# Expert layers of a decoder trunk: gathered expert rows replaced by dense products over both expert tables with a sparse gate matrix

## The chip, the cores and the metric

One core of a Trainium2 chip runs the whole program in one launch. The metric is the device time of that core in microseconds (us), lower is better. All data and all products are float32.

## The reference

The input is 256 tokens of width 1024; 16 learned meta tokens go in front, so there are 272 rows, worked on as a tile of 16 and two tiles of 128. Two layers follow, each an attention and then an expert feed-forward ("PEER"). The attention parts are not what the change is about. The expert part is, cut to what matters:

```python
q = (xt @ w_q).reshape(n, 8, 2, 128)                       # 8 heads, two halves
s = jnp.einsum('nhcd,ckd->nhck', q, subkeys)               # 128 keys per half
s_top, i_top = lax.top_k(s, 16)
cand = s_top[:, :, 0, :, None] + s_top[:, :, 1, None, :]   # 16 x 16 pairs
cand_id = i_top[:, :, 0, :, None] * 128 + i_top[:, :, 1, None, :]
best, pick = lax.top_k(cand..., 16)                        # 16 experts per head
ids = ...; g = jax.nn.softmax(best, axis=-1)
act = gelu(einsum('cd,ced->ce', xc, u[ids])) * g           # u, v: (16384, 1024) per layer
out = einsum('ce,ced->cd', act, v[ids])
```

Each token picks 8 x 16 = 128 of the 16384 experts of its layer. For each pick it needs one row of `u` (a dot product with the token) and one row of `v` (added to the output with weight `act`). Each table of a layer is 64 MiB.

## The kernel before, in words

The engines run hand-written instruction streams that meet only at semaphores. Tokens of the expert part are taken in groups of 16 (`GT = 16`): 8 groups for each tile of 128 and one for the meta tokens, and since the meta tokens are not needed after layer 0, there are 17 + 16 = 33 groups. In a group, partition p stands for (head, token), 8 x 16 = 128 pairs, and the 16 picks of a pair are walked one after the other (k = 0 to 15).

For pick k of a group, GpSimd starts an indirect DMA that fetches 128 rows of `u` (one per partition, 4 KB each), and the same for `v` of the group before (`gather`, L505). The arena is a ring of 8 slots for `u` and 8 for `v`. VectorE multiplies the fetched rows with the tokens' rows and sums (`step`, L1077). ScalarE applies gelu and writes 16 diagonal-like matrices (L764), and TensorE multiplies each with the fetched rows of `v`, 2 x 512 columns per pick, into two PSUM banks (`v_sum`, L1371). In the middle of a group (k = 7, `ROUTE`) the next group is routed: TensorE makes the scores, VectorE finds the best keys and pairs (L1014 to L1064).

The other work is spread into the gaps between the picks by a table (`work`): while tile 1 of a layer is in its expert groups, tile 2's attention, output projection and query projection run, and so on across the layers. So only tile 1's attention of layer 0 stands ahead of the first group, some 140 us. The weights come in blocks of 0.5 MB through a ring of six slots on SyncE's queue.

Of the kernel before, what the change touches and what calls it, by code (L numbers as in the profile page):

```python
# [5 lines left out]
F32 = mybir.dt.float32  # L22
U32 = mybir.dt.uint32
# [8 lines left out]
TILES = 3  # L32
# [11 lines left out]
EXPERTS = 16384  # L44
NKEYS = 128
SEL = 16
GT = 16
# [8 lines left out]
WB = 6  # L56

XC = META + P

UP_STEPS = 15  # L60


class Chain:

    def __init__(self, eng, sem):
        self.eng, self.sem, self.n, self.off = eng, sem, 0, 0

    def do(self, ins):  # L70
        self.n += 1
        ins.then_inc(self.sem, 1)
        self.eng.wait_ge(self.sem, self.n + self.off)


def build(nc, x, meta, a_norm, a_w_in, a_q_norm, a_k_norm, a_w_o, kv_norm, kv_w, b_norm, b_w_q, b_w_o,
          ffn_norm, peer_w_q, peer_subkeys, peer_u, peer_v, rope, out):
    u_rows = peer_u.rearrange("l e d -> (l e) d")
    v_rows = peer_v.rearrange("l e d -> (l e) d")
    with ExitStack() as ctx:  # L80
        def sb(name, cols, dt=F32, rows=P):
            return ctx.enter_context(nc.sbuf_tensor(name, [rows, cols], dt))
# [11 lines left out]
        arena = sb("arena", 16 * D)  # L94
        ring = arena[:, :].rearrange("p (k d) -> p k d", d=D)

        w_r = arena[:, 0:KC * (A_COLS - Q_COLS)].rearrange("p (c n) -> p c n", n=A_COLS - Q_COLS)
        w_q = arena[:, 8 * D:8 * D + KC * Q_COLS].rearrange("p (c n) -> p c n", n=Q_COLS)

        wb_t = sb("weight_blocks", WB * D)  # L100
        wb = wb_t[:, :].rearrange("p (s c n) -> p s c n", s=WB, n=P)

        hx_t = sb("residual", TILES * D)
        hx = hx_t[:, :].rearrange("p (i d) -> p i d", d=D)
        x1_t = sb("x_norm_T", KC * XC)
        xT = x1_t[:, :].rearrange("p (c n) -> p c n", n=XC)
        x2_t = sb("kv_norm_T", KC * XC)
        xT2 = x2_t[:, :].rearrange("p (c n) -> p c n", n=XC)
        qt_t = sb("queries_T", 2 * 17 * P)


        QT = qt_t[:, :].rearrange("p (c g m) -> p c g m", c=2, m=P)
        QTw = qt_t[:, :].rearrange("p (c g h t) -> p c g h t", c=2, h=HEADS, t=GT)
        dg_t = sb("diagonals", 16 * P)
        DG = dg_t[:, :].rearrange("p (k m) -> p k m", m=P)
        l_t = sb("logits", GROUP * T)
        L = l_t[:, :].rearrange("p (h k) -> p h k", k=T)
        re_t = sb("index_scores_and_softplus", 2 * GROUP * T)
        r_t, e_t = re_t[:, 0:GROUP * T], re_t[:, GROUP * T:2 * GROUP * T]
        E4 = e_t.rearrange("p (h k) -> p h k", k=T)  # L120
        SC, WK = e_t[:, 0:T], e_t[:, T:2 * T]
        R4 = r_t.rearrange("p (h k) -> p h k", k=T)
        C4 = R4
        q_t = [sb("q_T0", HEADS * META), sb("q_T1", HEADS * P), sb("q_T2", HEADS * P)]
        qT = [a[:, :].rearrange("p (h n) -> p h n", h=HEADS) for a in q_t]
        pt_t = sb("weights_T", 3 * 512)
        PT = pt_t[:, :].rearrange("p (j m) -> p j m", m=512)
        TMP = pt_t[:, 0:1280]
        o_t = [sb("heads_T0", HEADS * META), sb("heads_T", HEADS * P)]
        oT = [a[:, :].rearrange("p (h n) -> p h n", h=HEADS) for a in o_t]  # L130
        oT = [oT[0], oT[1], oT[1]]


        PJ = {(1, "all"): qt_t[:, 0:1920], (0, "k"): qt_t[:, 1920:3840], (0, "q"): o_t[1][:, 0:Q_COLS],
              (2, "k"): re_t[:, 256:2176], (2, "q"): re_t[:, 256:2176]}
        PJ = {k: a.rearrange("p (b d) -> p b d", d=P) for k, a in PJ.items()}
        XR = sb("x_rows", D)
        XH = sb("x_norm", D)
        grow = [sb(f"ffn_gain_row{l}", D) for l in range(2)]
        V_t = sb("values", TILES * 256)  # L140
        V = V_t[:, :].rearrange("p (i d) -> p i d", d=256)
        kT_t = sb("keys_T", KV * T)
        kT = kT_t[:, :].rearrange("p (g k) -> p g k", k=T)
        kiT = sb("index_keys_T", T)
        qi_t = [None, sb("index_queries_T1", 2 * P), sb("index_queries_T2", 2 * P)]
        qiT = [None] + [a[:, :].rearrange("p (a n) -> p a n", n=P) for a in qi_t[1:]]
        WI_t = sb("index_weights", TILES * IDX_HEADS)
        WI = WI_t[:, :].rearrange("p (i h) -> p i h", i=TILES)
        BIAS = sb("bias", T)
        BIAS0 = sb("bias_T0", META)  # L150

        LATER = sb("later", T + 1)
        rope_t = sb("rope", TILES * 48)
        RO = rope_t[:, :].rearrange("p (i c) -> p i c", c=48)
        qg = sb("q_gain", P)
        kg = sb("k_gain", P)
        g_rows = XR[:, 512:640]
        gcol = sb("gain_columns", 40)
        sk_rows = XR[:, 0:512].rearrange("p (m d) -> p m d", d=P)
# [3 lines left out]
        zeros = sb("zeros", P)  # L163
        ones = sb("ones", 1)
        iota16 = sb("iota16", SEL)
        spread = XR[:, 640:880]
# [1262 lines left out]
```

## Time and profile before

| what | value |
|---|---|
| time, median of 3 runs | 1856.72 us (1853.03 to 1862.37) |
| span of the profiled execution, first to last instruction | 2039.2 us |
| mean granted TensorE clock in it | 0.909 |
| TensorE matmul busy | 1538.2 us, 75% |
| VectorE busy | 1112.9 us, 55% |
| GpSimd busy | 1224.5 us, 60% |
| DMA: bytes moved, mean rate | 628.89 MB, 308 GB/s |

How to read it: the profiled execution's span is 9.8% above the median of the timed runs; its own time beside the span is not given, so the span stands for it. Busy time of TensorE has two parts that overlap, matmul (PE) and weight load (PEld). A float32 matmul shows as two records, each with a weight load of its own. The DMA share is the mean busy share of the core's 16 DMA engines.

### The profile page before, as it was taken

The numbers are of one execution on the slowest core, as the hardware profiler recorded it, in microseconds if no ns is written. First come the engines' busy times: TensorE is split into PE (matmuls) and PEld (weight loads), VectorE is DVE, ScalarE is ACT, GpSimd is POOL, SyncE is SP. The second block draws the span as 40 slices with busy tenths as digits, with TensorE's granted clock in tenths as the row PEclk, the third lists the DMA queues.
The fourth block names the chain that finished last, engine by engine and source line by source line (L and its number), as shares of the span: only waits on it lengthen the run. The fifth ranks groups of instructions, "written<-read, shape, count | busy, mean of one in ns | idle before, by whom it ended". The sixth has DMA issues, their size and how long they took to land. (4 is left out here: it accounts for less than half of the span.)

```text
span 2039.2 us, 16883 instructions
## 1 busy us (share of the span) xinstructions
PE 1538.2 (75%) x5028; PEld 777.5 (38%) x5028; DVE 1112.9 (55%) x2785; ACT 409.9 (20%) x1031; POOL 1224.5 (60%) x1073
## 2 busy tenths in 40 slices
PE   7786767896876778869687688769687667666668
PEld 3572323454542245425353244335354222222223
DVE  2648756626445563655645545675545545555551
ACT  2122211113211122321222112331222101111111
POOL 0007767765546676766656656766656656666664
PEclk9898899998989989989799999889798998888889
DMA  7277888997888899989989899979988878888887
GB/s 263 57 192 264 315 297 308 331 369 244 302 312 326 322 335 385 343 304 345 360 299 361 316 328 356 357 283 331 365 297 301 322 299 328 329 320 296 291 292 292
DMA packets 281342, 628.89 MB, mean 308 GB/s; under 512 B 19576, under 2 KB 143264, under 8 KB 281264
## 3 DMA queue, kind: packets, MB, share of 16 engines
q0 software_dynamic: 152064, 553.72, 73.5%
q1 hardware_dynamic: 129200, 74.22, 12.5%
q8 instruction: 39, 0.64, 0.1%
q14 instruction: 39, 0.32, 0.0%
HBM read 626.81 MB, written 1.05 MB: 308 GB/s over the span
## 5 line engine op out<-in xcount | busy, mean ns | idle before, releaser
L1371 PE MATMUL banks<-arena,diagonals 128*128 128x512 f32 x2112 | 1061.8, 639 | 339.9 <-ACT diagonals L764 149.7
L505 POOL DMA_INDIRECT arena<-in_peer_u_dram,ids_u x528 | 590.4, 1118 | 615.4 <-DVE arena L1077 238.5
L1077 DVE SCALAR_TENSOR_TENSOR arena<-arena,x_rows 128x1024 f32<-128x1024 f32 x528 | 623.6, 1223 | 235.5 <-DMA arena<-in_peer_u_dram,ids_u 216.8
L505 POOL DMA_INDIRECT arena<-in_peer_v_dram,ids_v x528 | 630.5, 1194 | 181.5 <-issue 142.7
L1371 PEld LDWEIGHTS banks<-arena,diagonals 128*128 128x128 f32 x2112 | 394.9, 202 | 893.3 <-issue 757.4
L1014 DVE MAX8 top_values<-scores 128x8 f32<-128x128 f32 x66 | 16.1, 285 | 341.2 <-ACT scores L733 208.2
L764 ACT ACTIVATE diagonals<-select_group,activations 128x128 f32<-128x128 f32 x528 | 158.6, 393 | 12.2 <-PE banks L1371 8.1
L1268 PEld LDWEIGHTS banks<-x_norm_T,weight_blocks 128*128 128x128 f32 x1024 | 130.0, 198 | 27.3 <-issue 27.3
L1268 PE MATMUL banks<-x_norm_T,weight_blocks 128*128 128x128 f32 (+1 forms) x1024 | 129.8, 284 | 1.0 <-issue 1.0
L1342 PE MATMUL banks<-residual,select_tokens 128*128 128x512 f32 (+1 forms) x132 | 72.2, 674 | 40.0 <-ACT select_tokens L726 23.3
L733 ACT ACTIVATE scores<-banks 128x256 f32<-128x256 f32 x33 | 12.7, 385 | 397.1 <-PE banks L1348 194.9
L752 ACT ACTIVATE gelu<-dots 128x16 f32<-128x16 f32 x33 | 7.2, 217 | 321.3 <-DVE arena L1077 279.9
L647 ACT ACTIVATE queries_T<-banks 128x128 f32<-128x128 f32 (+1 forms) x64 | 17.9, 280 | 259.8 <-PE banks L1268 177.3
L1250 PEld LDWEIGHTS banks<-weight_blocks,heads_T 128*128 128x128 f32 x512 | 62.5, 195 | 15.3 <-issue 13.8
L1250 PE MATMUL banks<-weight_blocks,heads_T 128*128 128x128 f32 x512 | 63.1, 279 | 2.9 <-issue 2.2
L1342 PEld LDWEIGHTS banks<-residual,select_tokens 128*128 128x128 f32 (+1 forms) x132 | 25.8, 206 | 79.6 <-issue 43.1
L736 ACT ACTIVATE gate_exp<-best,minus_best 128x16 f32<-128x16 f32 x33 | 10.2, 308 | 219.9 <-DVE minus_best L1045 122.3
L1160 PE MATMUL banks<-arena,kv_norm_T 128*128 128x512 f32 (+3 forms) x128 | 47.1, 526 | 0.0
L1114 PE MATMUL banks<-ident,x_norm 128*128 128x128 f32 (+1 forms) x88 | 13.5, 304 | 43.4 <-ACT x_norm L577 42.6
L1092 DVE TENSOR_TENSOR activations<-gelu,gates 128x16 f32<-128x16 f32 x33 | 5.8, 175 | 73.5 <-ACT gelu L752 61.2
L1361 PE MATMUL banks<-zeros 128*128 128x512 f32 x20 | 17.8, 1041 | 36.1 <-DVE residual L1102 33.5
L1077 DVE DVE_READ_ACCUMULATOR arena<-arena,x_rows 128x1 f32 x528 | 43.3, 82 | 0.0
(211 smaller groups left out, 1088.2 us busy)
## 6 DMA issues: line engine op xcount, KB each, us to landing
weight_blocks<-in_peer_w_q_dram SPq DMA_DIRECT2D x64, 512.0 KB
arena<-in_peer_u_dram,ids_u POOLq DMA_INDIRECT x528
arena<-in_peer_v_dram,ids_v POOLq DMA_INDIRECT x528
weight_blocks<-in_a_w_o_dram SPq DMA_DIRECT2D x16, 512.0 KB
weight_blocks<-in_b_w_q_dram SPq DMA_DIRECT2D x16, 512.0 KB
weight_blocks<-in_b_w_o_dram SPq DMA_DIRECT2D x16, 512.0 KB
arena<-in_a_w_in_dram SPq DMA_DIRECT2D x8, 512.0 KB, 9.1
weight_blocks<-in_kv_w_dram SPq DMA_DIRECT2D x8, 512.0 KB
```

What stands on the lines that cost most here:

```text
L505: pool.indirect_dma_start(out=ring[:, slot, :], out_offset=None, in_=table, in_offset=bass.IndirectOffsetOnAxis(ap=ids[:, k:k + 1], axis=0 ...
L647: return A(dst, src, ACT.Copy)
L764: A(DG[:, k, :], SG[:, :], ACT.Copy, scale=AV[:, k:k + 1]).then_inc(s_DG, 1)
L1014: ins = dve.max(top[:, 16 * h:16 * h + 8], S0[:, s])
L1077: stt(ring[:, slot, :], ring[:, slot, :], 1.0, XR[:, :], ALU.mult, ALU.mult, accum_out=DOT[:, k:k + 1]).then_inc(s_dots, 1)
L1114: return pe.transpose(dst, src, ident[:src.shape[0], :src.shape[0]])
L1160: ins = mm(bank[:n, b + m, :z - a], src[:, cc, o:o + n], w, start=cc == 0, stop=cc == KC - 1)
L1250: ins = mm(bank[:, 3 + 2 * (m // 4), d], oT[i][:, h, :], w[:, h, :], start=h == 0, stop=h == HEADS - 1)
L1268: ins = mm(bank[:, k, :w], ws[:, cc, :], xT[:, cc, o:o + w], start=cc == 0, stop=cc == KC - 1)
L1342: ins = mm(bank[:, m, :], XS[:nt, :], hx[:nt, i, 512 * m:512 * m + 512], start=True, stop=True)
L1361: mm(bank[:, 6 + m, :].rearrange("p (a b) -> p a b", b=P), zeros[:, :], zeros[:, :].unsqueeze(1).broadcast_to([P, 4, P]), start=True, stop ...
L1371: ins = mm(bank[:, 6 + m, :], DG[:, k, :], ring[:, slot, 512 * m:512 * m + 512], start=False, stop=False, skip_group_check=True)
```

## The change

The expert part no longer fetches rows. Both tables of a layer are streamed once, in blocks, and all 16384 experts are computed for all tokens; a gate matrix that is zero wherever a token did not pick an expert sets what counts. Transposed activations (`hT`, `xT`: model width on partitions, tokens along the row) are used throughout. In each layer:

- `u` comes 1 MB (256 experts) at a time through a ring of three slots, each MB as four transfers of 32 partitions by 8 pieces of 1 KB. VectorE transposes each half (128 experts) in 32 x 32 squares (`lift`, three buffers). `dots` multiplies: 8 matmuls of 272 columns (256 in layer 1) for each of 128 blocks; ScalarE's gelu moves the result into `M`, a matrix of 16384 x 272 that lies in SBUF.
- Routing runs on VectorE inside the first half of that loop (`route`), between the transposes, for whole tiles of 128 tokens at once.
- The gate matrix: per token and per half of the first key, one matmul of 64 columns of two one-hot matrices (`group`). GpSimd makes one of them, one instruction per token and half (`one_hots`); VectorE makes the other, eight tokens at once, and multiplies the result into `M` (`gate`). The first half of the keys is done inside the second half of `dots`, the second half inside the first half of `values`.
- `values` multiplies `v` (as weights, read with a step of 8 elements, `perm`) with `M`: 8 x 128 products of 272 columns in layer 0, each split in 144 + 128 columns, and of 256 columns in layer 1.

The small stages (projections, attention, output projection, query projection, scores) stand one after the other ahead of `dots` and between `values` of layer 0 and `dots` of layer 1, for all tiles together; nothing of them overlaps the expert part any more. The loop of the old groups is gone, all is written out.

```diff
-            def gather(table, ids, k, slot):
-                pool.indirect_dma_start(
-                    out=ring[:, slot, :], out_offset=None, in_=table,
-                    in_offset=bass.IndirectOffsetOnAxis(ap=ids[:, k:k + 1], axis=0)).then_inc(s_ld[slot], 16)
...
+                elif kind in ("u0", "u1"):
+                    u = peer_u[int(kind[1])][256 * s:256 * s + 256, :]
+                    for a in range(4):
+                        sp.dma_start(to[32 * a:32 * a + 32, :].rearrange("p (r n) -> p r n", r=8),
+                                     u[:, 256 * a:256 * a + 256].rearrange("(r i) n -> i r n", i=32)).then_inc(got, 16)
...
+                    for t in range(GT):
+                        at = GT * q + t
+                        ins = pool.tensor_scalar(LW[:, gg % 2, t, :], iota[:, :], IDT[:, 1, at:at + 1],
+                                                 IDT[:, 2, at:at + 1], ALU.is_equal, ALU.mult)
+                    ins.then_inc(s_L, 1)
...
-                    stt(ring[:, slot, :], ring[:, slot, :], 1.0, XR[:, :], ALU.mult, ALU.mult,
-                        accum_out=DOT[:, k:k + 1]).then_inc(s_dots, 1)
...
+            def lift(l, b):
+                gb, n = NKEYS * l + b, FIRST[("u0", "u1")[l]] + b // 2
+                dve.wait_ge(s_slot[n % SLOTS], LANDED[n])
+                if gb >= LIFTED:
+                    dve.wait_ge(s_dot, gb - LIFTED + 1)
+                dve.transpose(lifted[:, gb % LIFTED, :].rearrange("p (c r i) -> p c r i", c=KC, r=4),
+                              ring[:, n % SLOTS, D * (b % 2):D * (b % 2) + D].rearrange("p (r j c) -> p c r j", r=4, c=KC)).then_inc(s_lift, 1)
...
-                for m in range(2):
-                    ins = mm(bank[:, 6 + m, :], DG[:, k, :], ring[:, slot, 512 * m:512 * m + 512],
-                             start=False, stop=False, skip_group_check=True)
-                ins.then_inc(s_vused, 1)
...
+                for t in range(GT):
+                    ins = mm(gate_out(gg)[:, :, t], LW[:, gg % 2, t, :], RW[:, gg % 2, t, :], start=True, stop=True)
+                ins.then_inc(s_g, 1)
...
+                    for m in range(KC):
+                        ins = mm(bank[:, b % DOTB, :T - lo], u[:, m], xT[:, m, lo:], start=m == 0, stop=m == KC - 1)
+                    ins.then_inc(s_dot, 1)
...
+                    for m in range(KC):
+                        for a, z, to in v_out(l, m):
+                            ins = mm(to, perm(w[:, b % 2, :], m), M[:, b, a:z], start=False, stop=b == NKEYS - 1, skip_group_check=True)
```

Three places where the order shows the change. First TensorE in the expert part before: the products of the gathered `v` rows, with other stages' matmuls in the gaps and the next group's routing (L1342, L1348).

```order
L1371 MATMUL banks<-arena,diagonals 128x512 x4
L1268 MATMUL banks<-x_norm_T,weight_blocks 128x144 x8
L1371 MATMUL banks<-arena,diagonals 128x512 x2
L1342 MATMUL banks<-residual,select_tokens 128x512 x2
L1348 MATMUL banks<-subkeys_T,group_queries_T 128x128 x2
```

And TensorE in the changed kernel, from the end of `dots` of layer 0 to the start of `values` (the small gate products are L1114, `experts` is the matrix `M`).

```order
L1114 MATMUL banks<-one_hot 128x64 x8
L1140 MATMUL banks<-x_norm_T,lifted 128x272 x16
L1114 MATMUL banks<-one_hot 128x64 x8
L1140 MATMUL banks<-x_norm_T,lifted 128x272 x8
L1114 MATMUL banks<-one_hot 128x64 x8
L1140 MATMUL banks<-x_norm_T,lifted 128x272 x32
L1152 MATMUL banks<-zeros,ident 128x512 x5
L1161 MATMUL banks<-experts,ring 128x144
L1161 MATMUL banks<-experts,ring 128x128
```

The 512-column products are gone, and products of 272, 144 + 128 and 64 columns stand in their place. No other stage's matmul is left between them.

Second, VectorE in the expert part before: eight products with fetched rows on either side of the change of group.

```order
L1077 SCALAR_TENSOR_TENSOR arena,dots<-arena,x_rows 128x1024 x8
L1092 TENSOR_TENSOR activations<-gelu,gates 128x16
L1071 TENSOR_TENSOR x_rows<-banks,ffn_gain_row 128x1024
L1077 SCALAR_TENSOR_TENSOR arena,dots<-arena,x_rows 128x1024 x8
```

And VectorE in the changed kernel at the last pair search of a tile and its decode. L776 is the transpose (`lift`) that a block of TensorE's products waits for.

```order
L776 STREAM_TRANSPOSE lifted<-ring 128x1024
L812 TENSOR_TENSOR experts<-experts 128x128
L814 TENSOR_SCALAR experts<-experts 128x128
L815 TENSOR_SCALAR experts<-experts 128x128
L816 CAST experts<-experts 128x256
L817 CAST experts<-experts 128x256
L822 TENSOR_TENSOR experts<-experts,iota 128x2048
L824 TENSOR_TENSOR experts<-experts 128x2048
L826 TENSOR_REDUCE experts<-experts 128x128
L822 TENSOR_TENSOR experts<-experts,iota 128x2048
L824 TENSOR_TENSOR experts<-experts 128x2048
...
```

The decode of a whole tile stands between two transposes, with six operations over 2048 elements and nothing for TensorE among them.

## Rows read from the trace of the kernel before

**Rows 1.** Cores view, and the page's busy times by engine.

```profile
core 0: 2039.2 us, clock 0.909
PE 1538.2 (75%) x5028; PEld 777.5 (38%) x5028; DVE 1112.9 (55%) x2785; ACT 409.9 (20%) x1031; POOL 1224.5 (60%) x1073
```

**Rows 2.** Windows: span, each engine's busy us (instructions), PEclk, DMA share, GB/s.

```profile
700.00:900.00 200.00, 155.13 (x535) 79.83 (x534) 125.69 (x300) 56.53 (x133) 134.35 (x114) 0.93 0.92 331
900.00:1100.00 200.00, 164.06 (x647) 94.85 (x645) 98.39 (x259) 37.19 (x100) 126.34 (x113) 0.91 0.96 345
```

**Rows 3.** DMA queues: packets, MB, share of the 16 engines.

```profile
q0 software_dynamic: 152064, 553.72, 73.5%
q1 hardware_dynamic: 129200, 74.22, 12.5%
```

**Rows 4.** Page, costliest groups: busy us, mean ns, idle before and releaser.

```profile
L1371 PE MATMUL banks<-arena,diagonals 128*128 128x512 f32 x2112 | 1061.8, 639 | 339.9 <-ACT diagonals L764 149.7
L505 POOL DMA_INDIRECT arena<-in_peer_u_dram,ids_u x528 | 590.4, 1118 | 615.4 <-DVE arena L1077 238.5
L1077 DVE SCALAR_TENSOR_TENSOR arena<-arena,x_rows 128x1024 f32<-128x1024 f32 x528 | 623.6, 1223 | 235.5 <-DMA arena<-in_peer_u_dram,ids_u 216.8
```

**Rows 5.** Timeline, TensorE: start, duration, operation, records (two per matmul).

```profile
15.33 8.71 PE L1160 MATMUL banks<-arena,x_norm_T 128*128 128x512 f32 x16 [0.78 <-DVE x_norm_T L812]
...
44.36 7.93 PE L1160 MATMUL banks<-arena,kv_norm_T 128*16 128x512 f32 x32
...
68.07 11.39 PE L1160 MATMUL banks<-arena,kv_norm_T 128*128 128x512 f32 x32
...
87.27 7.41 PE L1250 MATMUL banks<-weight_blocks,heads_T 128*128 128x128 f32 x64 [0.69 <-ACT heads_T L641]
```

**Rows 6.** Windows inside three dense stretches.

```profile
68.20:79.20 11.00, 11.00 (x33) 5.76 (x31) 10.31 (x30) 1.37 (x2) 0.00 (x0) 1.00 0.00 0
87.40:94.60 7.20, 7.20 (x64) 7.09 (x64) 3.72 (x22) 1.32 (x2) 0.00 (x0) 1.00 0.44 127
95.50:102.60 7.10, 7.10 (x65) 7.02 (x63) 0.95 (x3) 0.00 (x0) 0.00 (x0) 1.00 0.99 277
```

**Rows 7.** Timeline, TensorE: transposes of 16 rows, one record each.

```profile
727.13 0.66 PE L1114 MATMUL banks<-ident,x_norm 16*128 16x16 f32 x8 [0.84 <-issue]
```

**Rows 8.** Lines by form, VectorE: busy us, mean ns.

```profile
L1014 DVE MAX8 top_values<-scores 128x8 f32<-128x128 f32 x66 | 16.1, 285 | 341.2 <-ACT scores L733 208.2 <-issue 133.0
...
L1019 DVE FIND_INDEX8 top_index<-top_values,scores 128x8 uint32<-128x128 f32 x66 | 18.9, 287 | 0.0
L1020 DVE MATCH_REPLACE8 scores_left<-top_values,scores 128x128 f32<-128x128 f32 x66 | 18.4, 278 | 0.0
...
L1041 DVE MAX8 best<-scores_left 128x8 f32<-128x256 f32 x33 | 14.1, 428 | 20.4 <-remote 13.3 <-DVE scores_left L1039 5.1 <-issue 1.1
...
L1053 DVE TENSOR_TENSOR one_hot<-pick_f,iota 128x512 f32<-128x512 f32 x33 | 22.9, 694 | 5.7 <-DVE pick_f L1051 4.3 <-issue 0.5
...
L1071 DVE TENSOR_TENSOR x_rows<-banks,ffn_gain_row 128x1024 f32<-128x1024 f32 x33 | 40.4, 1223 | 2.4 <-DVE activations L1092 1.6
```

**Rows 9.** Lines by form, GpSimd and ScalarE.

```profile
L498 POOL TENSOR_SCALAR_AFFINE_SELECT later<-later 128x273 f32<-128x273 f32 x1 | 0.4, 416 | 0.0
...
L489 POOL TENSOR_SCALAR_AFFINE_SELECT ident<-ident 128x128 f32<-128x128 f32 x1 | 0.3, 295 | 0.2 <-POOL iota L486 0.2
...
L733 ACT ACTIVATE scores<-banks 128x256 f32<-128x256 f32 x33 | 12.7, 385 | 397.1 <-PE banks L1348 194.9 <-issue 144.3 <-remote 58.0
```

**Rows 10.** Timeline, VectorE: first and last step of one tile's head norms and rotation.

```profile
45.92 1.49 DVE L853 TENSOR_TENSOR weights_T<-queries_T 128x1280 f32<-128x1280 f32 x1 [0.62 <-ACT index_weights L592]
...
55.55 0.32 DVE L828 TENSOR_TENSOR queries_T<-weights_T 128x160 f32<-128x160 f32 x1
```

**Rows 11.** Timeline, VectorE: first and last softplus step, tile 2, one half of the heads.

```profile
1290.95 1.29 DVE L934 TENSOR_SCALAR logits<-banks 128x1088 f32<-128x1088 f32 x1 [5.80 <-issue]
...
1303.75 1.29 DVE L961 TENSOR_TENSOR logits<-logits,later 128x1088 f32<-128x1088 f32 x1
```

More of the change, by code:

```diff
@@ L189, in build @@
[L189 to L203 removed]
+        iota = sb("iota", P)
+        one = sb("ones", 1)
@@ L431, in gaps, with turn_out @@
-        def gaps(steps, l, i, j, slot):
-            if number(j):
-                for k, name, *what in work.get((l, i, j), ()):
-                    if k == slot and name in steps:
-                        steps[name](*what)
+            return bank[:n, 4 - 4 * g:8 - 4 * g, :keys]
+        def turn_out(i, g, j, rows):
+            n = NT[i]
+            if i == 0:
+                return bank[:rows, 6 + g, 0:64]
+            return bank[:rows, (2 * g if i == 1 else 4 - 4 * g) + j, :GROUP * n]
@@ L766, in _ @@
-            route(*GROUPS[0])
-            walk(act, step, c, 1)
+            for g in range(2):
+                turned(0, 0, g)
+                pv(0, 0, g)
+            for g in range(2):
+                exp(2, g)
+            for g in range(2):
+                turned(0, 2, g)
+                pv(0, 2, g)
+            norm(1)
+            queries(0)
+            scores(0)
+            gelus(0)
+            norm(2)
+            act.wait_ge(s_kv, 1)
+            A(kT[:, :, :], bank[:, 0:2, :T], ACT.Copy).then_inc(s_kva, 1)
@@ L770, in _ @@
+            for g in range(2):
+                turned(1, 2, g)
+                pv(1, 2, g)
+            norm(3)
+            queries(1)
+            scores(1)
+            gelus(1)
+            for i in (1, 2):
+                act.wait_ge(s_ot, 2 * i - 1)
+                A(halves(i, 0), out_bank(i, 0), ACT.Copy).then_inc(s_fina, 1)
         @block.vector
@@ new lines, in _ @@
+            for g in range(2):
+                soft_b(0, 2, g)
+            for g in range(2):
+                turned(0, 2, g)
+            res(0)
+            norm(1)
+            queries(0)
+            experts(0)
+            norm(2)
+            dve.wait_ge(s_kv, 1)
+            for i in range(3):
+                ins = dve.tensor_copy(V[:NT[i], i, :], bank[:NT[i], 2 + i, 0:256])
+            ins.then_inc(s_kvd, 1)
+            dve.wait_ge(s_later, 2)
+            soft_a(1, 1, 0)
+            soft_a(1, 1, 1)
@@ new lines, in _ @@
+            soft_a(1, 2, 0)
+            for g in range(2):
+                soft_b(1, 1, g)
+            for g in range(2):
+                turned(1, 1, g)
+            soft_a(1, 2, 1)
+            for g in range(2):
+                soft_b(1, 2, g)
+            for g in range(2):
+                turned(1, 2, g)
+            res(1)
+            norm(3)
+            queries(1)
+            experts(1)
+            for i in (1, 2):
+                dve.wait_ge(s_ot, 2 * i)
+                dve.tensor_copy(halves(i, 1), out_bank(i, 1)).then_inc(s_find, 1)
@@ L1375, in step @@
-            def step(l, i, j, par):
-                n = group_no(l, i, j)
-                last = before(l, i, j)
-                for k in range(16):
-                    if last:
-                        v_sum(n - 1, k)
-                    if number(j) and any(s == k and name in IN_ROW_BANKS for s, name, *_ in work.get((l, i, j), ())):
-                        pe.wait_ge(s_xru, n + 1)
-                    gaps(gap, l, i, j, k)
-                    if k == ROUTE and after(l, i, j):
-                        route(*after(l, i, j))
-                if not last or ends(*last):
-                    clear(l, i)
```

1717 lines of the change are left out of this document (856 added, 861 removed).

## The prediction

> **What bounds the kernel now.** I read the busy times first [rows 1], then windows in the steady part [rows 2], then the costliest groups and the DMA queues [rows 3, 4]. No compute engine is full: TensorE's matmuls take 75% of the span, GpSimd 60%, VectorE 55%. The 16 DMA engines are at 0.92 and 0.96 in the two windows, with 331 and 345 GB/s [rows 2]. The gathers are 553.72 of the 628 MB [rows 3], which is 2 x 528 x 128 rows x 4 KB, so the expert rows fill the DMA engines; the most frequent releaser of VectorE's dot products is the landing of `u` rows, 216.8 of 235.5 us [rows 4]. Transfers set the pace, and TensorE is next.
>
> The change halves the bytes: four tables of 67.1 MB are 268 MB, and with some 40 MB of weights 308 MB; at 331 GB/s that is 930 us, if transfers stayed the bound. They don't, and the whole prediction is a count of TensorE's columns.
>
> **What a float32 column costs.** I looked for stretches in which TensorE has one kind of matmul and no gap [rows 5]. At 68.07 us, 16 matmuls (32 records) of 512 and 324 columns in turn, 6,688 columns, take 11.39 us: 1.70 ns a column. At 87.27 us, 32 matmuls of 128 columns take 7.41 us: 231 ns each. The granted clock is 1.00 in both, the 2.4 GHz level [rows 6]. Both fit four cycles a column plus 15 ns a matmul: 4 x 418 / 2.4 + 15 = 712 ns against 11.39 / 16 = 712, and 213 + 15 = 228 against 231. So a product costs 469 ns at 272 columns, 442 at 256, 255 at 144, 228 at 128.
>
> **The sum.**
> - *The four dense products.* `dots` of layer 0: 1,024 x 469 ns = 480 us. `dots` of layer 1: 1,024 x 442 = 452. `values` of layer 0 is split, and I take it that each part loads its weights anew: 1,024 x (255 + 228) = 495. `values` of layer 1: 452. Together **1,879 us**. That alone exceeds today's median. It can be seen without the fit: before, the products with `v` stream 1,056 x 512 = 540,672 columns in 1,061.8 busy us [rows 4]; the new ones stream 1,081,344, exactly twice as many, because the dot products too now go to TensorE and all 16384 experts are computed.
> - *Gate products*: 544 + 512 = 1,056 of 64 columns, and each loads 128 columns of weights. No row has this pair. Without the load it would be 107 + 15 = 122 ns; the stretch at 44.36 us supports it (eight of 512 and eight of 64 columns with 16-column weights: 7.93 us, and the fit gives 7.92 [rows 5]). In the 128-column stretch the weight load is busy 7.09 of 7.20 us [rows 6], so two loads may themselves take up to 225 ns; 16-column transposes with one 128-column load come every 83 ns [rows 7], so two might take 165. I take 228, the row with the same weights: **241 us**. Bounds: 122 (112 less) and 456 (twice, 241 more), the latter because the result is written to PSUM with a step of eight elements, which no row shows.
> - *Start to `dots` of layer 0.* First product at 15.33 us before [rows 5]; here all three tiles are transposed and normalised first: 20. Projection of all tiles, 42,560 columns in 96 matmuls: 72. Attention, now bare: head norms and rotation take 10 us of VectorE per tile [rows 10], three tiles in a row on its queue, the first one's behind the 21 us of tile 0's projection; then the top-64 selection, the softmax, transposes and value products of two full tiles in turn; laid end to end 85. Output projection 64 x 469 ns = 30, norm 12, query projection 128 x 469 ns = 60, scores, their copies and the first transpose 14. Together **293**; before, the first group started near 142.
> - *Between the layers*, all of it hidden in gaps before and bare now: residual and norm 13, shared keys and values 18 (10,496 columns), queries 28, stick-breaking attention 55 (the softplus chain of tile 2 takes 14 us per half of the heads [rows 11], tile 1 some 8, plus products), output projection 28, norm 8, query projection 57, scores and first transpose 12: **219**.
> - *VectorE's stalls.* A block of `dots` lasts 3.75 us (3.54 in layer 1). Best keys of a head: four MAX8 at 0.24, four FIND_INDEX8 at 0.29, two MATCH_REPLACE8 at 0.28 us, their match loads and waits, 3.4 us; with two transposes at 1.22 (the 1024-element row [rows 8]) 5.8 per two blocks, hidden. A best-pairs step 2.7 plus one transpose is 3.9 per block, level with TensorE. The decode of a tile is not hidden: 2048 elements cost 2.28 us (from 694 and 1,223 ns at 512 and 1024), six of them and some small ones are 17 us with no transpose between, and at most three blocks, some 9.5 us, are lifted ahead. TensorE then stands 9 us, four times in all, the meta tokens' routing adds 5, and the two starts a little: **50**.
> - *Two turns from `dots` to `values`* (clearing five or four banks with 512-column products, last gates): **14**. *End* (last sums, transposes, output): **15**.
>
> Sum: 1,879 + 241 + 293 + 219 + 50 + 14 + 15 = **2,711 us**, and I predict 2,710. The sum is one of profiled durations. Before, the span is 9.8% above the timed median [rows 1]. I don't scale mine down: the dense rate is four cycles at the granted clock, so nothing of the recording is in it; where before's excess comes from is not shown, and scaling all would give 2,470.
>
> **What stays hidden.** *The `u` and `v` streams*: 1 MB per two blocks, 1.05 MB in 7.5 us, needs 140 GB/s; weights came at 277 GB/s in the last stretch of [rows 6]. *GpSimd's one-hot rows*: eight per group, and TensorE needs a group every 8.9 us (64 blocks and 34 groups in 303 us), so it binds only above 1.1 us an instruction; a 128-element instruction takes 295 ns, a 273-element one 416 [rows 9]. *ScalarE's gelu*: 385 ns for 256 elements [rows 9] against 3.5 us. *The transpose* has no row: at 0 it changes nothing, at twice 1.22 us the pair steps take 5.1 and the key steps 8.3 per two blocks, about 80 us more in both layers.
>
> **The rivals.**
> 1. *Weights with a step load slower* (22%): 2,860 to 3,200. `values` and the output projection read their weights with a step of eight elements; the trace has no such load. If it doubled the load, 222 ns (7.09 us for 32 products [rows 6]) becomes 444: level with 442 and below 469, so only the split `values` of layer 0 pays, 2,048 x 444 = 909 instead of 495, total 3,125; half as much extra load gives 2,900. Against it: at one step per column the load has slack unless it is bound by the read. The Trainium skill speaks for this rival: "Advanced Engine Details and Errata", Memory Cachelines, says that accesses to a different 16-byte line each pay a penalty, and "PSUM — Partial Sum Buffer", Specifications, that any non-contiguous pattern slows matmuls significantly, which would hit the gate products too. By them the sum would be the 3,125 and 241 more for the gates. Nothing in this trace shows either.
> 2. *The feed binds* (8%): 3,050 to 3,300. Each transfer of `u` reaches only 32 partitions in 1 KB pieces, so it may be far slower than the weight transfers. From 140 GB/s down it decides; at 70 GB/s a pair of blocks takes 15 us instead of 7.5 and `dots` grows by about 480 us a layer, at 100 GB/s by 190. The same place, if GpSimd's instruction took 1.5 us instead of 0.3: 12 us a group, about 100 us in each of four halves.
> 3. *Cheaper than summed* (8%): 2,440 to 2,550: gate products at 122 ns, no stalls, part of before's 9.8% in my rows too.
> 4. *Faster than before* (2%), the other side: dense streams that run below the four cycles. TensorE's four products take 1.74 ns a column in my sum; the total comes under 1,857 only if that falls by 854 us, to 0.95 ns. The stretches at 1.70 ns, gapless at clock 1.00, speak against it. The Trainium skill, "TensorE: Matmul & The Clock Gate", Back-to-back issue gap, gives a sustained 131 ns per 512-column matmul, less than its own isolated 216; four such passes would be 1.02 ns a column and the sum near 1,930. The trace contradicts it at 1.70.
>
> **The numbers.** Likeliest (58%): TensorE-bound, 2,550 to 2,860, from gates at 122 ns with stalls gone, up to transposes at twice the price or gates a third dearer and some waits that I missed. The range reaches up into rival 1, to 3,130, and holds 80%. Times within 0.5% of 1,857 (about what a measurement of this kernel can tell from no change) have 1%, faster 2%, slower 97%.
>
> **What would show it.** TensorE over 90% busy at clock near 1.00 from `dots` to the end of each layer; 8 products per block in 3.75 us; VectorE's decode the longest releaser of TensorE inside `dots`; DMA share near 0.4; products of 144 + 128 columns at 483 ns together. If instead the 128-column products of `values` in layer 0 take over 300 ns with the weight load busy throughout, it is rival 1; if TensorE waits for VectorE and VectorE for landings of `u`, rival 2. The prediction is wrong if the column cost is not that of the dense stretches, or if the bare stages, a fifth of the sum, were mis-sized by half.

## The result, and the profile after

The changed kernel takes 3258.22 us (median of 4 runs, 3255.68 to 3261.03). The kernel before takes 1855.43 (4 runs, 1853.03 to 1862.37). The ratio is 1.755, 95% interval 1.751 to 1.759. The forecast was 2,710 with a range of 2,550 to 3,130: the sign was right, and the time lies 548 us above the forecast and above the range. The kernel before itself is timed at two levels, on one chip too: 1,853 to 1,857 us, as here, and 2,016 to 2,030 us at a lower granted clock (0.91 to 0.92 against 0.95 to 0.96), so what follows compares times in us and gives a ratio only where the kernel before stood at the first level.

The page of the changed kernel: busy times, granted clock, the chain that ended last, and the costliest groups.

```profile
PE 3066.8 (94%) x14061; PEld 2802.7 (86%) x14061; DVE 1080.5 (33%) x1760; ACT 208.6 (6%) x428; POOL 869.6 (27%) x1083
...
PEclk9789999999999999999999997999999999999999
...
PE 88%; DVE 10%; ACT 1%; issue 0%; SPq 0%; DMA 0%; DVEq 0%
...
L1161 PE MATMUL banks<-experts,ring 128*128 128x144 f32 (+2 forms) x6144 | 1485.6, 403 | 0.0
L1161 PEld LDWEIGHTS banks<-experts,ring 128*128 128x128 f32 x6144 | 1473.3, 336 | 0.7 <-issue 0.5
L411 POOL TENSOR_SCALAR one_hot<-iota,ids_T 128x128 f32<-128x128 f32 x1056 | 864.4, 835 | 1276.7 <-PE banks L1114 798.3
L1140 PE MATMUL banks<-x_norm_T,lifted 128*128 128x272 f32 (+1 forms) x4096 | 942.6, 390 | 67.6 <-DVE lifted L776 66.2
L1140 PEld LDWEIGHTS banks<-x_norm_T,lifted 128*128 128x128 f32 x4096 | 777.7, 192 | 206.7 <-DVE lifted L776 74.9
L776 DVE STREAM_TRANSPOSE lifted<-ring 128x1024 f32<-128x1024 f32 x256 | 517.9, 2028 | 238.6 <-PE banks L1140 238.6
...
L1114 PEld LDWEIGHTS banks<-one_hot 128*128 128x128 f32 x2112 | 255.1, 192 | 5.2
L1114 PE MATMUL banks<-one_hot 128*128 128x64 f32 x2112 | 250.1, 272 | 0.0
```

Against [rows 1, 4], TensorE went from 75% to 94% busy, and no transfer stands in the chain any more. The row to stop at is the second L1161. Records of the same 128 x 128 load take 336 ns there and 192 ns in L1140. The weight load is busy in 1,473 of the 1,486 us that `values` has: these products wait for their weights and not for their columns. (A record's duration overlaps with its neighbours'; the price of a product is read below from one start to the next.)

Windows of the changed kernel by stage: `dots` and `values` of layer 0, the bare stages between the layers, and most of `dots` and `values` of layer 1 (columns as in [rows 2]).

```profile
296.70:871.60 574.90, 540.50 (x2604) 454.72 (x2604) 412.41 (x637) 61.69 (x141) 237.80 (x288) 0.97 0.53 118
871.60:1914.20 1042.60, 1042.53 (x4650) 1040.05 (x4650) 42.61 (x66) 0.02 (x1) 207.10 (x256) 1.00 0.19 64
1914.20:2150.00 235.80, 187.70 (x783) 149.03 (x783) 71.27 (x136) 48.89 (x75) 0.75 (x2) 0.87 0.28 85
2150.00:2700.00 550.00, 517.12 (x2604) 456.70 (x2603) 399.47 (x591) 56.67 (x137) 225.39 (x272) 0.98 0.55 123
2700.00:3230.00 530.00, 530.00 (x2475) 529.17 (x2474) 40.17 (x62) 0.00 (x0) 194.11 (x240) 1.00 0.35 121
```

Nearly all of the excess stands in one row: `values` of layer 0 takes 1,043 us where the sum had some 560 (495, half of the gate products, a turn). There the clock is 1.00 and both parts of TensorE are busy throughout. The dense products' pace is read from the timeline of the changed kernel, TensorE (start, duration, records, two per matmul):

```profile
584.68 7.55 PE L1140 MATMUL banks<-x_norm_T,lifted 128*128 128x272 f32 x32
592.07 1.89 PE L1114 MATMUL banks<-one_hot 128*128 128x64 f32 x16
...
892.97 15.48 PE L1161 MATMUL banks<-experts,ring 128*128 128x144 f32 x64
908.28 1.90 PE L1114 MATMUL banks<-one_hot 128*128 128x64 f32 x16
...
2711.83 7.99 PE L1161 MATMUL banks<-experts,ring 128*128 128x256 f32 x32
2719.66 1.90 PE L1114 MATMUL banks<-one_hot 128*128 128x64 f32 x16
```

From one start to the next, `dots` takes 7.39 us for 16 products, 462 ns each. The split products of `values` take 15.31 us for 32, 478 ns each, where 144 and 128 columns were to take 255 and 228. Layer 1's take 7.83 us for 16, 489 ns, where 256 columns were to take 442. Products of 478 ns with the weight load busy throughout are the sign that the prediction gave for its rival 1.

### The profile page after: what moved, and what is told of

The parts are those of the page before. It is cut to its first block, busy times and chain, and to the rows that moved or that the text cites. A ratio compares the mean times of both kernels' runs of the same rounds, so it can differ in the third digit from the quotient of the medians.

```text
span 3254.0 us, 33244 instructions
## 1 busy us (share of the span) xinstructions
PE 3066.8 (94%) x14061; PEld 2802.7 (86%) x14061; DVE 1080.5 (33%) x1760; ACT 208.6 (6%) x428; POOL 869.6 (27%) x1083
## 4 chain that ended last, share of the span: by engine, by line
PE 88%; DVE 10%; ACT 1%; issue 0%; SPq 0%; DMA 0%; DVEq 0%
PE banks L1161 45%; PE banks L1140 24%; PE banks L1114 7%; PE banks L1079 4%; DVE lifted L776 2%; PE banks L999 2%; PE banks L1058 2%; PE banks L1251 1%; PE banks L1048 1%; PE banks L981 1%; DVE experts L822 1%; DVE experts L824 1%; DVE experts L826 1%; PE banks L992 0%; DVE experts L804 0%; PE banks L1095 0%
## 5 line engine op out<-in xcount | busy, mean ns | idle before, releaser
L1161 PE MATMUL banks<-experts,ring 128*128 128x144 f32 (+2 forms) x6144 | 1485.6, 403 | 0.0
L1161 PEld LDWEIGHTS banks<-experts,ring 128*128 128x128 f32 x6144 | 1473.3, 336 | 0.7 <-issue 0.5
L411 POOL TENSOR_SCALAR one_hot<-iota,ids_T 128x128 f32<-128x128 f32 x1056 | 864.4, 835 | 1276.7 <-PE banks L1114 798.3
L1140 PE MATMUL banks<-x_norm_T,lifted 128*128 128x272 f32 (+1 forms) x4096 | 942.6, 390 | 67.6 <-DVE lifted L776 66.2
L1140 PEld LDWEIGHTS banks<-x_norm_T,lifted 128*128 128x128 f32 x4096 | 777.7, 192 | 206.7 <-DVE lifted L776 74.9
L776 DVE STREAM_TRANSPOSE lifted<-ring 128x1024 f32<-128x1024 f32 x256 | 517.9, 2028 | 238.6 <-PE banks L1140 238.6
L1114 PEld LDWEIGHTS banks<-one_hot 128*128 128x128 f32 x2112 | 255.1, 192 | 5.2
L1114 PE MATMUL banks<-one_hot 128*128 128x64 f32 x2112 | 250.1, 272 | 0.0
L543 ACT ACTIVATE experts<-banks 128x272 f32<-128x272 f32 (+1 forms) x256 | 100.1, 391 | 995.4 <-PE banks L1140 995.4
L1079 PE MATMUL banks<-x_norm_T,ring 128*128 128x272 f32 (+1 forms) x512 | 118.8, 395 | 10.9 <-DVE x_norm_T L632 10.3
L1058 PEld LDWEIGHTS banks<-experts,ring 128*128 128x128 f32 x256 | 61.5, 333 | 4.5 <-ACT experts L502 4.5
```

The source lines that it names most:

```text
L411: ins = pool.tensor_scalar(LW[:, gg % 2, t, :], iota[:, :], IDT[:, 1, at:at + 1], IDT[:, 2, at:at + 1], ALU.is_equal, ALU.mult)
L543: A(M[:, b, lo:], bank[:, b % DOTB, :T - lo], ACT.Gelu).then_inc(s_h, 1)
L776: dve.transpose(lifted[:, gb % LIFTED, :].rearrange("p (c r i) -> p c r i", c=KC, r=4), ring[:, n % SLOTS, D * (b % 2):D * (b % 2) + D].re ...
L1058: ins = mm(bank[:, m, :T - lo], perm(w[:, h % 2, :], m), oT[:, h, lo:], start=h == 0, stop=h == HEADS - 1)
L1079: ins = mm(bank[:, k, :T - lo], w[:, m % 2, P * k:P * k + P], xT[:, m, lo:], start=m == 0, stop=m == KC - 1)
L1114: ins = mm(gate_out(gg)[:, :, t], LW[:, gg % 2, t, :], RW[:, gg % 2, t, :], start=True, stop=True)
```

## The experiments

The first theory is rival 1, at another price: a weight load whose elements lie 32 bytes apart takes 478 ns per product, not 222, so it binds both the split products and those of 256 columns. The others are the gate products' output step, GpSimd, and the transposes. `e1_step1` to `e4_lift_plain` (which put the model's columns in another order) and `e9_gate64` (which leaves out half of the gates) are single runs; all others keep the whole computation (at a lower precision from experiment 5 on) and are medians of 4. Where nothing else is said, times are compared with the 3,258 us of the changed kernel, whose own runs lie within 5.4 us.

### 1. The step of the weights: 4, 8 and 16 bytes

```diff
-   ins = mm(to, perm(w[:, b % 2, :], m), M[:, b, a:z], ...)                                   # after: 32 bytes
+   ins = mm(to, w[:, b % 2, P * m:P * m + P], M[:, b, a:z], ...)                              # e1_step1: 4
+   ins = mm(to, w[:, b % 2, :].rearrange("p (q k c) -> p q c k", k=P, c=2)[:, m // 2, m % 2], ...)  # e2_step2: 8
+   ins = mm(to, w[:, b % 2, :].rearrange("p (q k c) -> p q c k", k=P, c=4)[:, m // 4, m % 4], ...)  # e3_step4: 16
```

> The changed kernel, but values reads its weights as eight runs of 128 adjacent elements instead of every eighth element (so the output columns come out in another order; the work is the same). Theory A, the step slows the weight load and nothing else: the split products of layer 0 fall from 484 to some 242 ns and the 256-column products of layer 1 from 489 to some 445, about 496 + 45 us in all, and the time goes from 3258 to about 2715 us. Theory B, the products are slow because of the gate matrix as moving operand, the five accumulating banks or the transfers of v beside them: no change, 3258 us.

> As e1_step1, with a step of two elements (8 bytes): four stretches of 256 elements, even and odd ones apart. If two reads for each 16-byte line are enough, as the Trainium skill (Advanced Engine Details and Errata, Memory Cachelines) says, the time is that of e1_step1, about 2715 us; if any step slows the load, 3258 us; if the cost grows with the bytes skipped, between.

> As e1_step1, with a step of four elements (16 bytes), a new 16-byte line for each element as with a step of eight. By the line rule all of the slowness is there: 3258 us. If the cost grows with the step, between e2_step2 and 3258.

Measured: 2,706.85, 2,715.26 and 3,220.75 us. Timeline and group of the first, then the load's group of the second and of the third:

```profile
886.85 7.71 PE L1161 MATMUL banks<-experts,ring 128*128 128x144 f32 x64
894.39 1.90 PE L1114 MATMUL banks<-one_hot 128*128 128x64 f32 x16
...
2204.78 7.13 PE L1161 MATMUL banks<-experts,ring 128*128 128x256 f32 x32
2211.75 1.89 PE L1114 MATMUL banks<-one_hot 128*128 128x64 f32 x16
...
L1161 PEld LDWEIGHTS banks<-experts,ring 128*128 128x128 f32 x6144 | 869.1, 191 | 52.2 <-issue 1.0
```

```profile
L1161 PEld LDWEIGHTS banks<-experts,ring 128*128 128x128 f32 x6144 | 893.9, 196 | 39.8 <-issue 1.0
```

```profile
L1161 PEld LDWEIGHTS banks<-experts,ring 128*128 128x128 f32 x6144 | 1440.4, 329 | 0.7 <-issue 0.5
```

One edit takes off 551 us, and the start-to-start times say where: 7.54 us for 32 split products (236 ns against 478, 2,048 times: 496 us) and 6.97 us for 16 of 256 columns (436 against 489, 1,024 times: 54 us). The sum is 550. Theory B falls with it, since `M`, the banks and the transfers of `v` are unchanged. The price is not proportional to the step: 191, 196, 329 and 336 ns at 4, 8, 16 and 32 bytes. It jumps where each element lies in a 16-byte line of its own. The Trainium skill, "Advanced Engine Details and Errata", Memory Cachelines, says just this: lines of 16 bytes, two hits on a line needed for full speed. The trace agrees, but for a rest: at 16 bytes a split product takes 468 ns (14.99 us for 32) and the whole 37 us less than at 32, which the rule does not give.

### 2. The same in the transposes

```diff
-   ring[:, n % SLOTS, ...].rearrange("p (r j c) -> p c r j", r=4, c=KC)).then_inc(s_lift, 1)
+   ring[:, n % SLOTS, ...].rearrange("p (c r j) -> p c r j", r=4, c=KC)).then_inc(s_lift, 1)
```

> The changed kernel, but VectorE's transposes read the ring in order instead of every eighth element (another order of the model's columns, so the output differs; same work). Theory A, the transpose takes 2.03 us because of the step: it falls to about 1.2 us, TensorE's waits for it in dots (66 + 33 us in the profile) fall to some 45 us, mostly the two decodes per layer, and the time by about 50 us to 3205. Theory B, the operation itself takes 2.03 us: no change, 3258 us.

Measured: 3,223.78 us, 34 less. The transposes' group, and TensorE's first wait:

```profile
L776 DVE STREAM_TRANSPOSE lifted<-ring 128x1024 f32<-128x1024 f32 x256 | 316.0, 1238 | 367.8 <-PE banks L1140 367.8
```

```profile
PE banks L1140 <- DVE lifted L776: 38.8, 5, 9.8
```

The transpose falls from 2,028 to 1,238 ns, and TensorE's waits for it from 66.2 to 38.8 us. Of VectorE's 202 us less in all, 34 show; the rest had been hidden. The expectation counted TensorE's waits as "66 + 33": the trace has 66.2 in both layers together, so 99 was 33 too many.

### 3. The gate products: output step, and the load

```diff
-   return bank[:, 5 + gg % GB, :].rearrange("p (k t) -> p k t", t=GT)
+   return bank[:, 5 + gg % GB, :].rearrange("p (t k) -> p k t", t=GT)                        # e6_gates
...
-   ins = mm(gate_out(gg)[:, :, t], LW[:, gg % 2, t, :], RW[:, gg % 2, t, :], ...)
+   ins = mm(gate_out(gg)[:64, :, t], LW[:, gg % 2, t, :64], RW[:, gg % 2, t, :], ...)        # e9_gate64
```

> The changed kernel, but the gate products write adjacent PSUM elements instead of every eighth one; VectorE reads them with a step when it multiplies them in. Computation unchanged. If a step in PSUM slows a product (the Trainium skill, PSUM, Specifications), the 64-column products fall from 217 ns towards 122 and the time by up to 100 us, to 3160. If they are bound by their weight load, nothing changes but VectorE's products: 3258 us.

> The changed kernel, but each gate product loads 64 weight columns instead of 128 and writes 64 partitions, so half of the gates are left out. If the 64-column products are bound by their two weight loads, they fall from 217 ns to some 122 to 130 (the 15 ns and four cycles a column of the dense stretches), 1056 x 0.09 = 95 us: 3160 us. If a fixed cost per product binds, 3258 us.

Measured: 3,256.72 us (3,255.58 to 3,258.79) and 3,186.12. The gate products of the second, timeline and group:

```profile
874.26 1.15 PE L1114 MATMUL banks<-one_hot 128*64 128x64 f32 x16
875.34 15.53 PE L1161 MATMUL banks<-experts,ring 128*128 128x144 f32 x64
...
L1114 PEld LDWEIGHTS banks<-one_hot 128*64 128x64 f32 x2112 | 132.9, 138 | 34.2 <-issue 21.4
```

With results written side by side the gate products have the same row as with a step of 32 bytes (250.1 us, 272 ns), and the time is the same. So no slowdown by PSUM's step is seen. With half the weight columns and as many streamed ones, eight products take 1.08 us instead of 1.73: 135 against 216 ns. So they are bound by the load of their 128 weight columns, as the choice of 228 over 122 assumed. (The edit also halves the partitions written; the two were not run apart. Of the 86 us that it takes off the products, the time shows 72.) This also limits the first result: a product that is already slow by its load could hide a slower write, up to 216 ns.

### 4. The full computation without the step: ScalarE copies

```diff
+   ins = A(lifted[:, gb % LIFTED, :].rearrange("p (c k) -> p c k", c=KC),
+           ring[:, n % SLOTS, ...].rearrange("p (k c) -> p c k", c=KC), ACT.Copy)
...
-   ins = mm(to, perm(w[:, b % 2, :], m), M[:, b, a:z], ...)
+   ins = mm(to, w[:, m], M[:, b, a:z], ...)
```

> The changed kernel with the whole computation kept: ScalarE, idle during values, copies each block of v out of the ring into adjacent order (the three buffers that the transposes use in dots), and TensorE reads its weights there. Theory A, the weight load's step is the whole miss and a copy of 1024 elements (some 1.05 us, or some 1.9 if the step slows ScalarE as well) hides behind a block of 3.5 to 3.9 us: 2710 to 2730 us, as with e1_step1. Rival: the copy competes or comes late at the start of values, and 50 us or more are left: 2770 or above.

Measured: 2,705.25 us (2,704.48 to 2,705.65). The copies:

```profile
L563 ACT ACTIVATE lifted<-ring 128x1024 f32<-128x1024 f32 x256 | 528.1, 2064 | 502.6 <-PE banks L1181 502.6
```

This is theory A, 5 us below its range, and the time of `e1_step1` with nothing left out. ScalarE reads with the step now, 2.06 us a block against 3.8 and 3.5 us of products, so all of it is hidden: 553 us for an engine that stood idle. To this, four transposes of each decode were moved from behind it to between its steps (`e10_spread`):

```diff
-   decode(l, i)
-   for _ in range(4):
-       lift(l, b)
+   todo += [b, b + 1, b + 2, b + 3]
+   decode(l, i, between)      # one lift after each step over 2048 elements
```

> e5_copied with the four transposes that follow each decode moved between its steps of 2048 elements; computation unchanged. The waits of TensorE for transposes are some 99 us in both layers, of which the four decodes are 56. If the 17 us without a transpose are their cause, most of the 56 us go: 2705 to 2655 us. If VectorE is simply full in the first half of dots (64 transposes at 2.03 and some 150 us of routing against 240 us of TensorE), the wait only moves to later blocks: 2690 to 2705.

```profile
PE banks L1169 <- DVE lifted L795: 38.0, 27, 4.1
```

Measured: 2,684.1 us (2,683.84 to 2,686.69), 21 less. TensorE waits 38.0 us for transposes (the row above) instead of 66.2, at most 4.1 at once instead of 14.1. Of the 56 us that the four decodes cost, 28 go from the waits and 21 from the time, less than the theory and more than its rival gave; the rest is now spread over shorter waits. (The 99 us of the expectation are 66.2 here too.) The ratio to the kernel before is 1.450 (1.443 to 1.457).

### 5. What remains is four float32 passes: bfloat16

From here on the expert products are in bfloat16, wholly or in part, so these kernels compute at a lower precision than both kernels compared. In `e7_bf16_values`, `M` and the copied `v` are bfloat16 (decode not spread).

> e5_copied, but M (the activations times the gates) and the copied v are written as bfloat16, so values multiplies in one pass instead of four; everything else stays float32. Theory A, TensorE's passes are the bound and nothing else in values is near: the products fall to at most 130 ns each and values is then held by ScalarE's copies, 2.06 us a block, 265 us a layer instead of some 550 and 510 with the gates: 2705 - 2 x 240 = 2200 to 2270 us. Rival, the transfers of v or the gate products hold it at once: above 2400 us.

Measured: 2,341.71 us (2,339.42 to 2,344.88), 72 above the range of theory A and below its rival. Waits of TensorE:

```profile
PE banks L1183 <- ACT lifted L565: 96.1, 119, 0.9
PE banks L1135 <- POOL one_hot L419: 91.9, 43, 3.4
```

In the half of `values` without gate products, a block (16 products in layer 0) takes TensorE 1.1 us, against 3.8 in float32, and comes every 1.93 us, close to the copy's 2.04. The second wait was not expected. GpSimd's one-hot instruction takes 0.83 us, not the 0.295 of [rows 9]; eight make 6.6 us. In the changed kernel that is under the 9 us that a group may take. Here 64 blocks of 1.93 us leave 34 groups 3.6 us each, and it is over. In that half of layer 0 (870 to 1,200 us) the granted clock is 0.85, where `e5_copied` has 1.00.

In `e11_bf16_all` the dot products are bfloat16 too, and the one-hot rows are split between GpSimd and VectorE. `e12_bf16_act` is its counterpart. **The expectation of `e12_bf16_act` misstates the edit**: the one-hot rows stay split there too, and it differs from `e11_bf16_all` only in that ScalarE makes all copies of `v`.

```diff
+   A(staged[...], ring[...].rearrange("p (k c) -> p c k", c=KC), ACT.Copy)   # u, to bfloat16
-   dve.transpose(lifted[...], ring[...].rearrange("p (r j c) -> p c r j", r=4, c=KC))
+   dve.transpose(lifted[:, gb % LIFTED, :], staged[:, gb % LIFTED, :])
```

> Every expert product in bfloat16 (the dot products too: ScalarE casts each block of u and writes it in adjacent order, VectorE transposes it, M, the tokens and the copied v are bfloat16), GpSimd makes the one-hot rows of the even groups and VectorE those of the odd ones, every third block of v is copied by VectorE, and the decode is spread as in e10_spread. Projections, attention, routing and gate products stay float32. Theory (the change loses because four float32 products of all experts cost TensorE four cycles a column, twice the columns of before; with one pass of bfloat16 they stop being the bound and other engines' turns are): 1,700 to 1,880 us, from 297 + 235 of bare stages, dots near 200 a layer if VectorE holds them and values 180 to 200. Rival (ScalarE binds: cast, gelu and copy together 2.45 us a block of dots, 314 us a layer): 1,950 to 2,050. A third: GpSimd still binds in the halves with gates, as in e7_bf16_values, then 2,100 or more.

> As e11_bf16_all, but GpSimd makes all one-hot rows (0.83 us an instruction, 6.6 us a group of eight) and ScalarE alone copies v. If the split of these two jobs is worth what e7_bf16_values suggests (34 groups of 6.6 us in each half, 224 us, against half of that), this run is 150 to 300 us slower than e11_bf16_all. If the dot products' cast on ScalarE is the bound, the two are within 60 us.

Measured: 1,925.07 (1,915.93 to 1,937.55) and 1,924.0 us (1,921.04 to 1,926.56). The ratio of the first is 1.039 (1.033 to 1.044). Waits of TensorE, windows (first and second half of `dots` of layer 0), timeline, and windows of its two groups of gate products in `e11_bf16_all`:

```profile
PE banks L1222 <- DVE lifted L832: 230.5, 117, 5.6
PE banks L1195 <- POOL one_hot L440: 100.7, 43, 5.1
PE banks L1243 <- ACT lifted L583: 66.0, 62, 3.1
...
303.00:505.00 202.00, 107.32 (x522) 61.78 (x523) 191.94 (x506) 156.57 (x141) 6.30 (x8) 0.65 0.78 163
505.00:691.00 186.00, 154.08 (x1061) 129.32 (x1060) 157.59 (x168) 145.95 (x130) 123.21 (x136) 0.83 0.86 183
...
530.69 3.68 PE L1195 MATMUL banks<-one_hot 128*128 128x64 f32 x16 [2.66 <-POOL one_hot L440]
534.16 3.55 PE L1222 MATMUL banks<-experts,lifted 128*128 128x272 bf16 x16
537.54 1.89 PE L1195 MATMUL banks<-one_hot 128*128 128x64 f32 x16
...
530.69:534.16 3.47, 3.47 (x17) 3.47 (x17) 2.96 (x3) 0.00 (x0) 0.00 (x0) 0.50 1.12 222
537.54:539.27 1.73, 1.73 (x18) 1.73 (x17) 0.69 (x1) 1.73 (x3) 1.73 (x3) 1.00 0.04 14
```

And waits of TensorE in `e12_bf16_act`:

```profile
PE banks L1243 <- ACT lifted L583: 97.4, 120, 0.9
PE banks L1195 <- POOL one_hot L440: 86.6, 43, 4.3
```

1,925 lies between the theory and its rival, so neither is borne out. VectorE holds the half of `dots` with the routing (192 of 202 us busy). In the second half no engine is busy for over 158 of the 186 us, and TensorE waits now for one, now for another; no run separates them. A new cost shows in the timeline: after a wait of 2.66 us eight gate products take 3.68 us, and a little later 1.89. The last two windows say why: the granted clock is 0.50 in the first, the 1.2 GHz level, and 1.00 in the second, the 2.4 GHz level. Who copies `v` makes no difference in time (1 us), but not because the copies cost nothing: in `e12_bf16_act` TensorE waits 97.4 us for them instead of 66.0 and 86.6 us for one-hot rows instead of 100.7. As its edit is not the one that its expectation speaks of, neither of that expectation's answers is tested.

`e13_bf16_gates` has three edits over `e11_bf16_all`:

```diff
-   LW = lw_t[:, :].rearrange("p (s t k) -> p s t k", s=2, t=GT)
+   LW = lw_t[:, :].bitcast(BF).rearrange("p (s t k) -> p s t k", s=HOTS, t=GT)    # HOTS = 4; RW alike
...
-   return SHARE and b % 3 == 2
+   return SHARE and (b % 3 == 2 if b < NKEYS // 2 else b % 2 == 1)
```

> As e11_bf16_all, with the two one-hot matrices of the gate products in bfloat16 as well (gates rounded to it), four buffers of each in place of two, and every second block of v copied by VectorE in the second half of values, where e11_bf16_all still waits for ScalarE. In e11_bf16_all a group of eight gate products takes TensorE 1.8 us and TensorE waits 100.7 us for GpSimd's one-hot rows in all. Theory (in the halves with gates TensorE's own weight loads and GpSimd's delivery set the pace): a group falls to under 1 us, up to 132 x 0.9 = 119 us of TensorE, of which part lands on VectorE and ScalarE, which are 76 to 83% busy there; waits for GpSimd halve: 1,790 to 1,870 us, so at or below the kernel before. Rival (those halves are held by VectorE's and ScalarE's own turns per block): 1,890 to 1,925.

Measured: 1,771.02 us (1,767.67 to 1,772.86), ratio 0.9545 (0.9507 to 0.9583): 4.6% faster than the kernel before, at a lower precision. It is also below what was expected. Page, chain and groups:

```profile
PE 1173.3 (66%) x7885; PEld 870.5 (49%) x7885; DVE 1140.7 (64%) x1998; ACT 1002.4 (57%) x836; POOL 579.2 (33%) x555
...
DVE 30%; PE 29%; POOL 14%; ACT 11%; DMA 8%; issue 7%; SPq 0%; DVEq 0%; POOLq 0%; ACTq 0%
...
L441 POOL TENSOR_SCALAR one_hot<-iota,ids_T 128x128 bf16<-128x128 f32 x528 | 574.1, 1099 | 682.5 <-ACT ids_T L565 428.4
...
L1196 PE MATMUL banks<-one_hot 128*128 128x64 bf16 x1056 | 99.9, 277 | 115.6 <-POOL one_hot L441 96.1
```

The gate products' busy time falls from 319 to 100 us. The waits for GpSimd hardly fall, 100.7 to 96.1, against the half that was expected, and those for transposes rise from 230.5 to 293.1: part of what TensorE gained it waits out elsewhere. `values` of layer 0 shrinks from 314 to 254 us and the second half of `dots` from 186 to 165. Which of the three edits brought how much stays open; they were not run apart. No engine is over 66% busy.

## Why the prediction failed, point by point

**The step that failed** is the third product of the sum's first term, the four dense products: "each part loads its weights anew: 1,024 x (255 + 228) = 495", with `values` of layer 1 at 452. It priced every product by its columns and took a load with a step of eight elements for a load of adjacent ones. Measured, 2,048 x 478 = 979 and 1,024 x 489 = 501 us, 533 above the 947 of the two. The runs show in its place that the load sets the pace: with adjacent weights and the same columns the products take 236 and 436 ns (experiment 1), and the full computation takes 2,705 us (experiment 4).

**Rival 1 had the mechanism** and a fifth of the chance, and its price was too low. It doubled 222 to 444 ns and found that "only the split `values` of layer 0 pays". Measured it is 478, over twice the 216 that a load-bound product takes with adjacent weights (experiment 3), and above the 442 of a 256-column product, so layer 1 pays too: 484 above the term in layer 0 and 49 in layer 1, 2,711 + 533 = 3,244 against the 3,254 of the span. The case against it was that a load at one step per column has slack unless the read binds. That was no measurement: no row had a load with a step. Of the two rules that the prediction quotes from the Trainium skill, the first, on 16-byte lines, was right, and the second, on PSUM, did not show (experiment 3).

**The rest of the sum held.** The kernel without the step is the test: 2,706.85 us against 2,711. It is a sum of small errors of both signs:

| term | predicted | measured, in the kernel with adjacent weights | 
|---|---|---|
| `dots`, both layers | 932 | 1,024 x (461 + 435 ns) = 918 |
| `values`, both layers | 947 | 2,048 x 236 + 1,024 x 436 = 930 |
| gate products | 241 | 1,056 x 216 ns = 228 |
| bare stages | 293 + 219 | 298 + 234 = 532 |
| VectorE's stalls | 50 | 66 |

The turns were forecast as 14 and are 9 (4.9 and 4.0), the end as 15 and is 10. The right column and these add up to 2,693; the span of that kernel is 2,705.1, and 12 us are in none of the parts. That the sum of 2,711 met 2,707 within 4 us is luck in part: too high by 54 (products, gates, turns, end), too low by 36 (bare stages, stalls), and those 12.

The columns cost four cycles and some 8 ns a product besides (461 ns against 453 at 272 columns); the 15 ns were too much, some 30 us in all.

**Transposes**: I took 1.22 us from a row of another operation and named twice that as the bound. It is 2.03 with the step; in order it is 1.24 (experiment 2). The stalls of 14 us per decode were forecast as 9.

**What was to stay hidden** stayed so, in one case by luck. The streams moved at 64 to 123 GB/s with the DMA share at or under 0.55, so rival 2 fell. GpSimd's instruction takes 0.835 us, nearly three times the row it was priced from, and below the 1.1 us from which it binds.

**The 9.8%**: I left my terms unscaled, and that was right; the changed kernel's profiled run (3,255.68 us) is within 3 us of its median. The excess of [rows 1] need not be the recording's: its span of 2,039 us at clock 0.909 lies close to the longer timings named with the result. The dense kernels keep their time there (3,256.72 us for `e6_gates`, beside 2,016 for the kernel before); why the gathers do not is open.

**Why the change loses at all** is as forecast: 1,081,344 columns at four cycles each. With the step gone and the decode spread, TensorE is still 94% busy and the time 2,684 us. In bfloat16 (`e13_bf16_gates`) the same plan needs less time than the gathers, but at a lower precision and with the work of the other engines shared out anew, so the share of the passes alone is not shown.

## What to carry to other kernels

Before a stream of matmuls is priced by its columns, read how the weights lie. Here a float32 product of up to 272 columns hid its load only while that load was at full speed, and with 16 or 32 bytes from one element to the next the load cost over twice as much (468 and 478 ns a product against 216). Give the step to an engine that is idle; ScalarE took it at no cost in time here. When a bound is removed, price every hidden instruction again from a row of its own operation, since the next bound is often one whose price never mattered.

## What was not expected of the hardware

- A step of 8 bytes in the weights costs next to nothing (196 against 191 ns a load record, 8 us in the whole), 16 bytes nearly as much as 32 (329, 336).
- VectorE's transpose of 1024 elements in float32 takes 1,238 ns in order and 2,028 with a step of 32 bytes. In bfloat16, in order, it takes 1,227: half the bytes save nothing.
- ScalarE's copy of 1024 elements with that step takes 2,064 ns; its operation on 1024 elements in order takes 1,052 in the kernel before (L573, `x_norm`). VectorE's copy with the step, to bfloat16, takes 1,085 (`e11_bf16_all`; 1,084 in `e13_bf16_gates`). The step costs VectorE's copy no more than 1024 elements cost in [rows 8], unlike its transpose.
- GpSimd's instruction on 128 elements with two scalars from memory takes 835 ns in the changed kernel, and 1,009 and 1,099 in `e11_bf16_all` and `e13_bf16_gates`, where VectorE is busy 58% and 64% of the time (in the last it also writes bfloat16). At 46%, in `e7_bf16_values`, it takes 828. Whether VectorE is the cause was not tested.
- In the bfloat16 kernels TensorE comes out of some waits of about 3 us at the 1.2 GHz level (in `e11_bf16_all`, after 2.66 us: clock 0.50, and 3.68 against 1.89 us for the same eight products).
